# Last expert of a decoder step: two row additions moved, ye copied by halves, scatter and squares by tile

## The chip, the cores and the metric

The kernel runs on one core of a Trainium2 chip. The metric is the device time of one execution in microseconds (us); lower is better. The runs of the kernel before are shown by their median and spread; the profile is of one further execution, which has a time of its own.

## The reference, cut to what matters

One inference step of a two-layer decoder trunk over 256 prompt tokens and 32 sample tokens (288 rows of 1024 numbers, float32). Only its last part is touched: the expert feed-forward of layer 1 and the final norm.

```python
def moe_swiglu(x, w_router, w_gate, w_up, w_down):
    logits = (x @ w_router).astype(jnp.float32)
    top_val, top_idx = lax.top_k(logits, TOP_K_EXPERTS)          # 2 of 8
    gate = jax.nn.softmax(top_val, axis=-1)
    combine = jnp.einsum('btk,btke->bte', gate, one_hot(top_idx, N_EXPERTS))
    for e in range(N_EXPERTS):                                    # D_FF = 2816
        out = out + combine[..., e:e + 1] * swiglu(x, w_gate[e], w_up[e], w_down[e])
x = x + moe_swiglu(rms_norm(x, norm_ffn_odd), ...)
y = rms_norm(x, norm_final)
```

## The kernel before, in words

Everything up to the router runs first (attention, convolution, dense feed-forward, RWKV mixing) and is not touched. The experts then run one after the other, e = 0 to 7, inside a loop over blocks of `CAP` = 96 rows per expert; with these inputs the loop makes one round. Each engine has its own instruction stream, written out by hand, and semaphores tie them together.

**One expert on TensorE** (`expert` in the tensor block) has six phases, each over one weight matrix half (1408 of the 2816 hidden columns): gate0, up0, gate1 (three `widen`, L1589, output to banks 0 to 2 or 3 to 5), down0 (`narrow`, L1606, banks 6 and 7), up1 (`widen`), and down1 (`narrow`). Between up1 and down1 TensorE gathers the next expert's rows (`gather`, L1557); for the last expert it instead transposes the table `give` (L1647), which says which row belongs to which token and with what share. Weights stream through three buffers `part` of eight pieces each, loaded by SyncE (L723) as the pieces of the phase three back come free.

**VectorE and ScalarE**: for each of two halves, ScalarE takes silu of the gate product (`sg2`, L2013), and VectorE's `hidden` multiplies it by the up product (`hp`, L2615) and transposes it (`hidT`, L2619); `narrow` waits for each of the three groups of `hidT` in turn. At the expert's end both copy its 96 result rows from banks 6 and 7 to `ye`, ScalarE columns 0 to 511 (L2019) and VectorE columns 512 to 1023 (L2639), six pieces of 32x256 each.

**Results of experts 0 to 6** go from `ye` to a table `expert_rows` in device memory. When the seventh has been written, GpSimd fetches for every token tile (two tiles of 128 tokens, one of 32) its rows by an indirect DMA, six gathers in all, two per tile, into two buffers `got` (L2865). VectorE adds each to the running sum `acc` (`rows_in`, L2597); a gather starts when the addition two before it has freed its buffer. In the last expert all six additions stand on VectorE ahead of `hidden(…, 0)`.

**The last expert's result** is not sent through memory: TensorE's `scatter` (L1573) multiplies `ye` by the transposed `give`, in six steps g of one tile and one half of the columns, order tile 0 left, tile 0 right, tile 1 left, and so on, into banks 3 to 5 in turn; VectorE's `add_rows` (L2608) adds each to `acc`, and a step from the fourth on waits until its bank has been added. After the sixth addition ScalarE squares and sums the three tiles (L2033), loads the table of the square root (L2036), and VectorE scales the rows to `y_out` (L2703), which SyncE writes out (L748, L751).

Two semaphores matter: `ye_ok` counts the copies to `ye` (one from each engine per expert), `sc_ok` the additions of `add_rows` (with one more from before the loop). `mix_ok` belongs to the RWKV stage and has come to 48 long before.

Of the kernel before, what the change touches and what calls it, by code (L numbers as in the profile page):

```python
# [155 lines left out]
def build(nc, I, O):  # L156
# [235 lines left out]
    OUT_0 = 7  # L392
    OUT_1 = OUT_0 + 2
    N_OUT = OUT_1 + 1 + KC + 1


    ident_in, x_in, cst_in, vec_in, x2_in = (
# [28 lines left out]
    gu_mm, silu_ok, hid_ok, down_mm, down_ok = sem("gu_mm"), sem("silu_ok"), sem("hid_ok"), sem("down_mm"), sem("down_ok")  # L426


    xx_ok, mix_ok, lh_mm, lh_ok = (sem(n) for n in ("xx_ok", "mix_ok", "lh_mm", "lh_ok"))
    el_ok, mask_ok, cum_ok, e_ok, kf_ok = (sem(n) for n in ("el_ok", "mask_ok", "cum_ok", "e_ok", "kf_ok"))  # L430
    t1_ok, sqk_ok, hs_mm, nk_ok, nsq_ok, rn_ok = (sem(n) for n in ("t1_ok", "sqk_ok", "hs_mm", "nk_ok", "nsq_ok", "rn_ok"))
    kk_mm, kk_ok, ab_ok, kd_ok, rr_ok = (sem(n) for n in ("kk_mm", "kk_ok", "ab_ok", "kd_ok", "rr_ok"))
# [323 lines left out]
    def _(pe):  # L756
# [340 lines left out]
        rms_pe(pe, 1, sq2)  # L1097
        h_in = [(0, HD), (1, HD), (2, P)]
        for i, r in h_in:
            pe.wait_ge(mix_ok, KC * (i + 1))  # L1100
            w = weights(pe, n0 + i)[:, 0:KC * r].rearrange("p (k n) -> p k n", k=KC)
            for k in range(KC):
                last = mm(bk[5 + i][0:r, 0:T], w[:, k], mx[:, i % 2, k], start=k == 0, stop=k == KC - 1)  # L1103
            last.then_inc(lh_mm, 1)
# [14 lines left out]
        def krv_job(j):  # L1119
            i = j // KC  # L1120
            pe.wait_ge(job_ok, NIN + max(j - 1, 24))
            pe.wait_ge(mix_ok, KC * (i + 1))
            project(pe, n0 + 3 + j - 24, mx[:, i % 2], bk[6 + j % 2][:, 0:T]).then_inc(job_mm, 1)

        for j in range(24, 33):
# [435 lines left out]

        def scatter(blk, g):

            if g == 0:
                pe.wait_ge(ye_ok, blk * (2 * NE) + 2 * NE)
                pe.wait_ge(gt_ok, blk + 1)
            if g >= 3:
                pe.wait_ge(sc_ok, blk * 6 + 1 + g - 2)
            i, half = g // 2, g % 2
            t0, tn = TILES[i]  # L1570
            for q in range(tn // 32):
                at = 32 * (q + half * (i == 2))
                last = mm(up_bk[g % 3][at:at + 32, :], giveT[:, t0 + 32 * q:t0 + 32 * q + 32],  # L1573
                          ye[:, 512 * half:512 * half + 512], start=True, stop=True)
            last.then_inc(sc_mm, 1)
# [39 lines left out]
        def expert(blk, e):  # L1615

            def gate0_k(k):
                if k == 0:
                    pe.wait_ge(xe_ok, blk * (2 * NE) + 2 * e + 2)

            def up0_k(k):
                if k == 0 and e == 0:
                    pe.wait_ge(sc_ok, blk * 6 + 1)

            def gate1_k(k):
                if k == 0:
                    pe.wait_ge(silu_ok, blk * (6 * NE) + FC + 6 * e + 3)

            def up1_k(k):
                if k == 0:  # L1630
                    pe.wait_ge(hid_ok, blk * (6 * NE) + FC + 6 * e + 3)

            widen(blk, e, 0, gate_bk, gu_mm, gate0_k)
            widen(blk, e, 1, up_bk, up_mm, up0_k)
            widen(blk, e, 2, gate_bk, gu_mm, gate1_k)
            if e:
                pe.wait_ge(ye_ok, blk * (2 * NE) + 2 * e)
            narrow(blk, e, 3, 0)
            widen(blk, e, 4, up_bk, up_mm, up1_k)

            pe.wait_ge(silu_ok, blk * (6 * NE) + FC + 6 * e + 6)
            pe.wait_ge(pick_ok, blk * NE + e + 2)
            if e < NE - 1:
                gather()
            else:
                for i, (t0, tn) in enumerate(TILES):
                    last = nc.tensor.transpose(gate_bk[2][0:CAP, t0:t0 + tn], give[0:tn, i], C["ident"][0:tn, 0:tn])  # L1647
                last.then_inc(gt_mm, 1)
            narrow(blk, e, 5, 1)
# [15 lines left out]
    def _(act):  # L1665
# [340 lines left out]
        def expert(blk, e):  # L2006
            for half in range(2):
                for g in range(3):
                    n = 6 * e + 3 * half + g
                    act.wait_ge(gu_mm, blk * (6 * NE) + FC + n + 1)  # L2010
                    if n >= 3:
                        act.wait_ge(hid_ok, blk * (6 * NE) + FC + n - 2)
                    nc.scalar.activation(sg2[:, g], gate_bk[g][:, 0:FQ], ACT.Silu).then_inc(silu_ok, 1)  # L2013
            act.wait_ge(down_mm, blk * (2 * NE) + FC + 2 * e + 2)
            if e:
                act.wait_ge(rows_out, blk * (16 * LAST) + 16 * e)
            for q in range(2):
                for g in range(3):
                    last = nc.scalar.copy(ye[32 * g:32 * g + 32, 256 * q:256 * q + 256],  # L2019
                                          down_bk[g // 2][32 * q:32 * q + 32, 256 * (g % 2):256 * (g % 2) + 256])  # L2020
            last.then_inc(ye_ok, 1)
            if e < LAST:
                act.wait_ge(ye_ok, blk * (2 * NE) + 2 * e + 2)
                act.dma_start(expert_rows[CAP * e:CAP * e + CAP, :], ye[:]).then_inc(rows_out, 16)

        act.wait_ge(blocks_ok, 1)
        n_blocks = act.value_load(blocks[0:1, 0:1], min_val=1, max_val=T // CAP)
        with act.Fori(0, n_blocks) as blk:
            for e in range(NE):
                expert(blk, e)  # L2030
        act.wait_ge(sc_ok, n_blocks * 6 + 1)
        for i, (t0, tn) in enumerate(TILES):
            last = nc.scalar.activation(y_out[0:tn, i], acc[0:tn, i], ACT.Square, accum_out=ssf[0:tn, i:i + 1])  # L2033
        last.then_inc(sq_ok, 1)
        act.wait_ge(ms_ok, 3)
# [4 lines left out]
    def _(dve):  # L2040
# [223 lines left out]
        def mixed(i, m):  # L2264
            for c in range(KC):
                v_ = VEC["mu"] + KC * m + c
                V.scalar_tensor_tensor(mx[:, i % 2, c], xx[:, c], vecT[:, v_:v_ + 1], xn2[:, c],
                                       ALU.mult, ALU.add).then_inc(mix_ok, 1)

        for i, m in enumerate((1, 4, 5, 2, 0)):  # L2270
            if i >= 2:
# [314 lines left out]
                                       share[r, i, bass.ds(blk * NE + e, 1)], ALU.is_equal, ALU.mult)  # L2586
            return last

        def rows_in(blk):

            for n in range(6):
                i, j = n // 2, n % 2
                tn = TILES[i][1]
                dve.wait_ge(rows_back[j], blk * 48 + 16 * i + 16)
# [5 lines left out]
        def add_rows(blk):  # L2600
            dve.wait_ge(spot_then_rows, blk * 7 + 7)
            for g in range(6):
                i, half = g // 2, g % 2
                tn = TILES[i][1]
                dve.wait_ge(sc_mm, blk * 6 + g + 1)
                a = acc[0:tn, i, 512 * half:512 * half + 512]
                at = 32 * half * (i == 2)
                V.tensor_tensor(a, up_bk[g % 3][at:at + tn, :], a, ALU.add).then_inc(sc_ok, 1)  # L2608
# [11 lines left out]

        def expert(blk, e):
            if e == LAST:
                rows_in(blk)
            hidden(blk, e, 0)
            if e == LAST:
                gives(blk, e)
            picks(blk, e + 1).then_inc(pick_ok, 1)
            hidden(blk, e, 1)
            if e < NE - 1:
                columns_in(blk, e + 1)  # L2630
# [3 lines left out]
            if e:  # L2634
                dve.wait_ge(rows_out, blk * (16 * LAST) + 16 * e)
            dve.wait_ge(down_mm, blk * (2 * NE) + FC + 2 * e + 2)
            for q in range(2, 4):
                for g in range(3):
                    last = V.tensor_copy(ye[32 * g:32 * g + 32, 256 * q:256 * q + 256],  # L2639
                                         down_bk[g // 2][32 * q:32 * q + 32, 256 * (g % 2):256 * (g % 2) + 256])  # L2640
            last.then_inc(ye_ok, 1)

        dve.wait_ge(rank_mm, 1)
        V.scalar_tensor_tensor(rank[:, 0:2, 0:NE], bk[0][:, 0:2 * NE].rearrange("p (i e) -> p i e", i=2), 1.0, sel[:, 0:2],
# [40 lines left out]
            last = V.tensor_copy(share[0:NS, 2, NE * b:NE * b + NE], comb[0:NS, 2])  # L2685
        link(last)
        dve.wait_ge(gn_pool, gp_at["acc1"])
        V.tensor_copy(blocks_f[0:1, 3:4], blocks_f[0:1, 1:2]).then_inc(sc_ok, 1)
        dve.wait_ge(blocks_ok, 1)
        n_blocks = dve.value_load(blocks[0:1, 0:1], min_val=1, max_val=T // CAP)  # L2690
        with dve.Fori(0, n_blocks) as blk:
# [216 lines left out]
```

## Time and profile before

| | |
|---|---|
| median of 3 runs | 1580.28 us (1578.26 to 1580.69) |
| the profiled execution | 1587.68 us, span of its instructions 1585.8 us |
| TensorE (PE) matmul busy | 1498.8 us, 95% of the span |
| VectorE (DVE), ScalarE (ACT), GpSimd (POOL) busy | 442.2, 220.9, 164.7 us |
| mean granted TensorE clock | 0.969 of full speed |
| DMA over the whole span | 384.86 MB, 243 GB/s |
| chain that ended last, by engine | PE 85%, DVE 9%, DMA 3%, ACT 1%, issue 1% |
| costliest group | L1589 matmul, 6144 instructions, 459.1 us |

The chain is the work that ended last, followed back from the end: at each step to what released it. Matmul records overlap, so the time of a stretch is read from starts, not from a sum of durations. "[2.81 <-DVE ye L2639]" behind a row says that the engine was idle for 2.81 us before it and what ended the idle time.

### The profile page before, as it was taken

What the parts mean: (1) busy time and instruction counts of PE and PEld (TensorE: products, weight loads), DVE (VectorE), ACT (ScalarE), POOL (GpSimd) and SP (SyncE); (2) the same over time, 40 slices, a digit from 0 to 9 for tenths busy, and PEclk for the clock granted to TensorE, in tenths of its full rate; (3) what the DMA queues carried; (4) which work ended last, traced back from release to release, by engine and by line L of the source; (5) the groups of instructions that cost most, each with busy time, mean ns of one, the idle gap of its engine ahead of it and who ended that gap; (6) DMA issues with size and microseconds to landing.
All of it is one profiled execution on the core that took longest, in us unless ns stands there. A gap on an engine that the chain in (4) does not pass through costs nothing.

```text
span 1585.8 us, 39125 instructions
## 1 busy us (share of the span) xinstructions
PE 1498.8 (95%) x17804; PEld 974.7 (61%) x17804; DVE 442.2 (28%) x962; ACT 220.9 (14%) x479; POOL 164.7 (10%) x208
## 2 busy tenths in 40 slices
PE   6999989999995998999899999999999999999985
PEld 4767877777773777889764555545454555545432
DVE  1289321111006456353631011211111011211123
ACT  3134120000002511131330000000000000000001
POOL 3127200000000224105200000000000000000100
PEclk9899999999997999998899999999999999999997
DMA  9636034353531430032489999999999999999992
GB/s 286 189 126 163 14 108 157 109 159 112 180 107 53 134 93 2 3 56 56 100 308 362 414 413 413 374 415 375 413 387 395 414 371 413 370 415 374 403 399 73
DMA packets 187551, 384.86 MB, mean 243 GB/s; under 512 B 42463, under 2 KB 125631, under 8 KB 187258
## 3 DMA queue, kind: packets, MB, share of 16 engines
q1 hardware_dynamic: 180352, 365.84, 62.6%
q0 software_dynamic: 3616, 12.85, 2.1%
q10 hardware_dynamic: 3418, 3.68, 0.7%
q8 instruction: 140, 2.29, 0.6%
q14 instruction: 25, 0.20, 0.0%
HBM read 375.59 MB, written 6.73 MB: 241 GB/s over the span
## 4 chain that ended last, share of the span: by engine, by line
PE 85%; DVE 9%; DMA 3%; ACT 1%; issue 1%; SPq 0%; DVEq 0%; POOL 0%; ACTq 0%; POOLq 0%
PE bk L1589 26%; PE bk L1606 14%; PE bk L1076 11%; PE bk L761 8%; PE bk L1089 5%; PE bk L1510 2%; PE bk L1557 2%; PE bk L1169 2%; PE bk L991 2%; DMA got<-expert_rows,spot_now 2%; DMA ring<-in_w_in_even 1%; PE bk L1103 1%; DVE left L2158 1%; DVE tops L2156 1%; PE bk L1113 1%
## 5 line engine op out<-in xcount | busy, mean ns | idle before, releaser
L1589 PE MATMUL bk<-part,xe 128*32 128x352 f32 x6144 | 459.1, 460 | 2.3 <-DVE xe L2580 2.3
L1589 PEld LDWEIGHTS bk<-part,xe 128*32 128x32 f32 x6144 | 207.1, 110 | 249.0 <-issue 246.5
L1606 PE MATMUL bk<-part,hidT 128*32 128x256 f32 x4224 | 234.7, 382 | 5.7 <-DVE hidT L2619 5.7
L1606 PEld LDWEIGHTS bk<-part,hidT 128*32 128x32 f32 x4224 | 141.5, 111 | 97.1 <-DVE hidT L2619 8.9
L1076 PE MATMUL bk<-xn,ring 128*128 128x288 f32 x704 | 173.8, 411 | 3.2 <-DMA ring<-in_ffn_up 3.2
L2615 DVE TENSOR_TENSOR hp<-sg,bk 128x352 f32<-128x352 f32 x48 | 37.5, 781 | 470.8 <-PE bk L1589 470.8
L1076 PEld LDWEIGHTS bk<-xn,ring 128*128 128x128 f32 x704 | 135.4, 192 | 41.2 <-issue 3.4
L761 PE MATMUL bk<-xg,ring 128*128 128x288 f32 x336 | 90.4, 429 | 9.9 <-DMA ring<-in_w_in_even 8.3
L761 PE MATMUL bk<-mx,ring 128*128 128x288 f32 x384 | 96.2, 409 | 0.0
L1089 PE MATMUL bk<-hid,ring 128*128 128x288 f32 x352 | 85.5, 406 | 0.0
L761 PEld LDWEIGHTS bk<-xg,ring 128*128 128x128 f32 x336 | 66.5, 201 | 30.3 <-issue 9.1
L761 PEld LDWEIGHTS bk<-mx,ring 128*128 128x128 f32 x384 | 72.0, 190 | 20.4 <-issue 0.9
L1089 PEld LDWEIGHTS bk<-hid,ring 128*128 128x128 f32 x352 | 66.9, 190 | 18.5
L2864 POOL TENSOR_TENSOR free_now<-row_ss 128x1 f32 x5 | 1.0, 195 | 668.4 <-DMA expert_rows<-ye 650.6
L2019 ACT COPY ye<-bk 32x256 f32<-32x256 f32 x48 | 17.4, 362 | 369.9 <-PE bk L1606 369.4
L2013 ACT ACTIVATE sg<-bk 128x352 f32<-128x352 f32 x48 | 22.2, 464 | 319.9 <-PE bk L1589 283.5
L2639 DVE COPY ye<-bk 32x256 f32<-32x256 f32 x48 | 20.3, 424 | 98.9 <-PE bk L1606 98.4
L2238 DVE TENSOR_TENSOR gs<-bk,rs 128x288 f32<-128x288 f32 x22 | 10.1, 458 | 132.5 <-PE bk L1076 132.5
L2787 POOL MEMSET rmask<- 128x288 f32 x1 | 0.3, 338 | 325.2 <-DVE xn L654 325.2
L1510 PE MATMUL bk<-gT,ro 128*128 128x288 f32 x128 | 34.1, 422 | 0.0
L1557 PE MATMUL bk<-xr,pick 128*32 128x256 f32 x576 | 32.6, 379 | 1.4 <-ACT Ss L1960 1.4
L1794 ACT ACTIVATE sg<-gs 128x288 f32<-128x288 f32 x22 | 9.8, 444 | 155.8 <-DVE gs L2238 155.8
(512 smaller groups left out, 1368.6 us busy)
## 6 DMA issues: line engine op xcount, KB each, us to landing
part<-in_moe_gate SPq DMA_DIRECT2D x136, 704.0 KB, 7.3
part<-in_moe_up SPq DMA_DIRECT2D x136, 704.0 KB
part<-in_moe_down SPq DMA_DIRECT2D x128, 704.0 KB, 8.3
ring<-in_rwkv_w_rkv SPq DMA_DIRECT2D x24, 512.0 KB, 3.9
ring<-in_ffn_gate SPq DMA_DIRECT2D x22, 512.0 KB, 5.6
ring<-in_ffn_up SPq DMA_DIRECT2D x22, 512.0 KB, 6.7
ring<-in_ffn_down SPq DMA_DIRECT2D x22, 512.0 KB, 4.2
ring<-in_w_in_even SPq DMA_DIRECT2D x16, 512.0 KB, 5.9
```

The lines of the kernel that those rows point to most:

```text
L761: last = mm(out, w[:, k], rhs[:, k], start=k == 0, stop=k == KC - 1)
L991: last = nc.tensor.matmul(bk[4 + c // 2][:, TP * (c % 2):TP * (c % 2) + TP], w[:, k], mixT[:, k, 0:TP], start=k == 0 and c % 2 == 0, stop= ...
L1076: last = mm(bk[2 * m + f % 2][:, 0:T], slots[2 * m + k // 4][:, k % 4, (f % 2) * P:(f % 2 + 1) * P], xn1[:, k], start=k == 0, stop=k == KC ...
L1089: last = mm(bk[banks[c]][:, 0:T], w[:, f % 2, c * P:(c + 1) * P], hid[:, f], start=f == 0, stop=f == FC - 1)
L1169: last = mm(bk[GRP[q % 3][par]][r, hp * CH:(hp + 1) * CH], lhs[r, p2, par, hp], rhs[r, p2, par, hp], start=True, stop=True)
L1510: last = mm(bk[OUT_BANK(c)][:, 0:T], w[:, k], gT[:, k], start=k == 0, stop=k == KC - 1)
L1557: last = mm(gate_bk[g // 2][32 * q:32 * q + 32, 256 * (g % 2):256 * (g % 2) + 256], pick[:, i, 32 * g:32 * g + 32], in_parts[:, q], start= ...
L1589: last = mm(banks[g][32 * c:32 * c + 32, 0:FQ], xe[:, k, 32 * g:32 * g + 32], parts[ph % 3][:, FH * k + FQ * c:FH * k + FQ * c + FQ], star ...
L1606: last = mm(down_bk[g // 2][32 * q:32 * q + 32, 256 * (g % 2):256 * (g % 2) + 256], hidT[:, half, g, 32 * m:32 * m + 32], parts[ph % 3][:, ...
L2013: nc.scalar.activation(sg2[:, g], gate_bk[g][:, 0:FQ], ACT.Silu).then_inc(silu_ok, 1)
L2615: V.tensor_tensor(hp[:, g].rearrange("p (m j) -> p j m", m=NM), sg2[:, g].rearrange("p (j m) -> p j m", m=NM), up_bk[g][:, 0:FQ].rearrange ...
L2639: last = V.tensor_copy(ye[32 * g:32 * g + 32, 256 * q:256 * q + 256], down_bk[g // 2][32 * q:32 * q + 32, 256 * (g % 2):256 * (g % 2) + 256])
```

## The change

Five things, all in or behind the last expert.

1. `rows_in` takes a range: additions 0 to 3 (the two big tiles) stay ahead of `hidden(…, 0)`, additions 4 and 5 (the tile of 32) come behind `give` and `pick`, ahead of `hidden(…, 1)`.
2. `ye` is copied half by half: each engine copies three pieces of the left 512 columns and then three of the right (ScalarE the even quarters, VectorE the odd). `ye_ok` now counts the left half; the right half is counted on `mix_ok`, renamed `mix_then_ye`, above the 48 (`MIXED`) that it had. This holds for all eight experts.
3. `scatter` goes left half of tiles 0 and 1, then right half of both, then tile 2 (`SCATTER`). Its first step waits for the left half of `ye` alone, its third for the right.
4. The squares start tile by tile, when the third, fourth and sixth addition is done (`DONE_AT`).
5. A square root of eight numbers into a part of `y_out` that is overwritten later stands ahead of the squares. The count of `sc_ok` before the loop is 6 in place of 1.

```diff
+    SCATTER = ((0, 0), (1, 0), (0, 1), (1, 1), (2, 0), (2, 1))
+    MIXED = 6 * KC
+    DONE_AT = (3, 4, 6)
...
         def scatter(blk, g):
 
+            i, half = SCATTER[g]
             if g == 0:
+                pe.wait_ge(gt_ok, blk + 1)
                 pe.wait_ge(ye_ok, blk * (2 * NE) + 2 * NE)
-                pe.wait_ge(gt_ok, blk + 1)
+            if g == 2:
+                pe.wait_ge(mix_then_ye, blk * (2 * NE) + MIXED + 2 * NE)
             if g >= 3:
-                pe.wait_ge(sc_ok, blk * 6 + 1 + g - 2)
-            i, half = g // 2, g % 2
+                pe.wait_ge(sc_ok, blk * 6 + 6 + g - 2)
...
             if e:
                 pe.wait_ge(ye_ok, blk * (2 * NE) + 2 * e)
+                pe.wait_ge(mix_then_ye, blk * (2 * NE) + MIXED + 2 * e)
             narrow(blk, e, 3, 0)
...
-            for q in range(2):
+            for half in range(2):
+                q = 2 * half
                 for g in range(3):
                     last = nc.scalar.copy(ye[32 * g:32 * g + 32, 256 * q:256 * q + 256],
                                           down_bk[g // 2][32 * q:32 * q + 32, 256 * (g % 2):256 * (g % 2) + 256])
-            last.then_inc(ye_ok, 1)
+                last.then_inc((ye_ok, mix_then_ye)[half], 1)
             if e < LAST:
                 act.wait_ge(ye_ok, blk * (2 * NE) + 2 * e + 2)
+                act.wait_ge(mix_then_ye, blk * (2 * NE) + MIXED + 2 * e + 2)
...
         act.wait_ge(sc_ok, n_blocks * 6 + 1)
+        nc.scalar.activation(y_out[32:64, 2, 0:NE], C["slots"][32:64, 0:NE], ACT.Sqrt)
         for i, (t0, tn) in enumerate(TILES):
+            act.wait_ge(sc_ok, n_blocks * 6 + DONE_AT[i])
             last = nc.scalar.activation(y_out[0:tn, i], acc[0:tn, i], ACT.Square, accum_out=ssf[0:tn, i:i + 1])
...
-        def rows_in(blk):
-
-            for n in range(6):
+        def rows_in(blk, first, last_):
+
+            for n in range(first, last_):
...
             for g in range(6):
-                i, half = g // 2, g % 2
+                i, half = SCATTER[g]
...
             if e == LAST:
-                rows_in(blk)
+                rows_in(blk, 0, 4)
             hidden(blk, e, 0)
             if e == LAST:
                 gives(blk, e)
             picks(blk, e + 1).then_inc(pick_ok, 1)
+            if e == LAST:
+                rows_in(blk, 4, 6)
             hidden(blk, e, 1)
...
-            for q in range(2, 4):
+            for half in range(2):
+                q = 2 * half + 1
                 for g in range(3):
                     last = V.tensor_copy(ye[32 * g:32 * g + 32, 256 * q:256 * q + 256],
                                          down_bk[g // 2][32 * q:32 * q + 32, 256 * (g % 2):256 * (g % 2) + 256])
-            last.then_inc(ye_ok, 1)
+                last.then_inc((ye_ok, mix_then_ye)[half], 1)
...
-        V.tensor_copy(blocks_f[0:1, 3:4], blocks_f[0:1, 1:2]).then_inc(sc_ok, 1)
+        V.tensor_copy(blocks_f[0:1, 3:4], blocks_f[0:1, 1:2]).then_inc(sc_ok, 6)
```

How the instructions stand now. On VectorE, in the last expert, from the additions of gathered rows on; before (`acc<-got` is an addition of gathered rows, `hp` and `hidT` the first half's hidden columns):

```order
L2597 SCALAR_TENSOR_TENSOR acc<-got,weight,acc 128x1024
L2597 ISA
L2597 SCALAR_TENSOR_TENSOR acc<-got,weight,acc 32x1024
L2596 REGISTER_ALU
L2597 ISA
L2597 SCALAR_TENSOR_TENSOR acc<-got,weight,acc 32x1024
L2613 REGISTER_ALU
L2615 TENSOR_TENSOR hp<-sg_200,bk 128x32x11
L2619 STREAM_TRANSPOSE hidT<-hp 128x352
```

and in the change, from the fourth addition to the second half's first product:

```order
L2607 SCALAR_TENSOR_TENSOR acc<-got,weight,acc 128x1024
L2623 REGISTER_ALU
L2625 TENSOR_TENSOR hp<-sg_200,bk 128x32x11
L2629 STREAM_TRANSPOSE hidT<-hp 128x352
```

```order
L2578 TENSOR_SCALAR pick<-cst,rank,ssf 128x96
L2607 ISA
L2607 SCALAR_TENSOR_TENSOR acc<-got,weight,acc 32x1024
L2606 REGISTER_ALU
L2607 ISA
L2607 SCALAR_TENSOR_TENSOR acc<-got,weight,acc 32x1024
L2623 REGISTER_ALU
L2625 TENSOR_TENSOR hp<-sg_200,bk 128x32x11
```

The two additions of 32 rows have moved from ahead of the first half's three products to behind `give` and `pick`.

On ScalarE, from the last copies to `ye` to the end of its stream, with the semaphores that each instruction waits for; before:

```order
L2019 COPY ye<-bk 32x256 x5
L2028 REGISTER_ALU
L2028 COMPARE_AND_BRANCH
L2031 ISA
L2033 ACTIVATE y_out,ssf<-acc 128x1024 [waits sc_ok]
L2033 ACTIVATE y_out,ssf<-acc 128x1024
L2033 ACTIVATE y_out,ssf<-acc 32x1024
L2036 ACT_TABLE_LOAD
L2036 ACTIVATE ssf<-ssf 128x3 [waits ms_ok]
```

and in the change:

```order
L2026 COPY ye<-bk 32x256 x5
L2036 REGISTER_ALU
L2036 COMPARE_AND_BRANCH
L2039 ISA
L2040 ACT_TABLE_LOAD
L2040 ACTIVATE y_out<-cst 32x8 [waits sc_ok]
L2042 REGISTER_ALU
L2043 ACTIVATE y_out,ssf<-acc 128x1024 [waits sc_ok]
L2042 REGISTER_ALU
L2043 ACTIVATE y_out,ssf<-acc 128x1024 [waits sc_ok]
L2042 REGISTER_ALU
L2043 ACTIVATE y_out,ssf<-acc 32x1024 [waits sc_ok]
```

The table load has moved ahead of the squares, right behind the copies and itself without a wait, and no other load stands between the squares and the last square root.

## Rows read from the trace of the kernel before

**Rows 1.** The waits, 1400 to 1586 us: engine, line, waited for, us, times, longest

```profile
PE bk L1606 <- DVE hidT L2619: 5.7, 5, 4.0
PE bk L1573 <- DVE ye L2639: 2.8, 1, 2.8
```

**Rows 2.** The chain in order of time: start us, us, what

```profile
1419.02 14.24 PE bk L1606 x264
```

**Rows 3.** Instructions in order of time, TensorE: start us, us, engine, line, operation

```profile
1465.41 42.79 PE L1589 MATMUL bk<-part,xe 128*32 128x352 f32 x576
1512.15 0.89 PE L1606 MATMUL bk<-part,hidT 128*32 128x256 f32 x8 [3.95 <-DVE hidT L2619]
...
1514.64 15.83 PE L1606 MATMUL bk<-part,hidT 128*32 128x256 f32 x248 [0.15 <-DVE hidT L2619]
1530.30 14.37 PE L1589 MATMUL bk<-part,xe 128*32 128x352 f32 x192
```

**Rows 4.** Instructions in order of time, VectorE, last expert

```profile
1500.53 1.29 DVE L2597 SCALAR_TENSOR_TENSOR acc<-got,weight,acc 128x1024 f32<-128x1024 f32 x1 [1.82 <-DMA got<-expert_rows,spot_now]
...
1509.46 1.27 DVE L2597 SCALAR_TENSOR_TENSOR acc<-got,weight,acc 32x1024 f32<-32x1024 f32 x1 [1.58 <-DMA got<-expert_rows,spot_now]
1510.77 0.75 DVE L2615 TENSOR_TENSOR hp<-sg,bk 128x352 f32<-128x352 f32 x1
...
1515.19 0.79 DVE L2568 TENSOR_SCALAR pick<-cst,rank,ssf 128x96 f32<-128x96 f32 x3
```

**Rows 5.** Instructions in order of time, GpSimd: the last gather

```profile
1502.65 0.87 POOL L2865 DMA_INDIRECT got<-expert_rows,spot_now  x1 [0.46 <-issue]
```

**Rows 6.** Instructions in order of time, SyncE's queue, last weights; and the tile part, 1462 to 1586

```profile
1481.63 12.75 SPq L723 DMA_DIRECT2D part<-in_moe_up  x8
1495.83 12.75 SPq L723 DMA_DIRECT2D part<-in_moe_down  x8
...
DMA to landing us min/median/max: 6.0/13.2/15.2
```

**Rows 7.** Instructions in order of time, the end of the kernel

```profile
1561.24 2.61 DVE L2639 COPY ye<-bk 32x256 f32<-32x256 f32 x6 [13.37 <-PE bk L1606]
...
1563.98 7.67 PE L1573 MATMUL bk<-ye,giveT 96*32 96x512 f32 x36 [2.81 <-DVE ye L2639]
...
1566.05 0.69 DVE L2608 TENSOR_TENSOR acc<-bk,acc 128x512 f32<-128x512 f32 x1 [2.20 <-PE bk L1573]
1567.68 0.69 DVE L2608 TENSOR_TENSOR acc<-bk,acc 128x512 f32<-128x512 f32 x1 [0.94 <-PE bk L1573]
...
1570.87 2.20 DVE L2608 TENSOR_TENSOR acc<-bk,acc 128x512 f32<-128x512 f32 x3 [0.79 <-PE bk L1573]
...
1575.20 1.04 ACT L2033 ACTIVATE y_out<-acc 32x1024 f32<-32x1024 f32 x1
...
1576.35 1.28 ACT L2036 ACT_TABLE_LOAD   x1
1576.36 0.17 DVE L2698 TENSOR_SCALAR ssf<-ssf 128x3 f32<-128x3 f32 x1 [3.29 <-ACT y_out L2033]
1577.65 0.20 ACT L2036 ACTIVATE ssf<-ssf 128x3 f32<-128x3 f32 x1
```

**Rows 8.** Stretches: us, PE, PEld, DVE, ACT, POOL busy (instructions), PEclk, DMA share, GB/s

```profile
1512.00:1514.60 2.60, 1.97 (x16) 0.36 (x16) 2.53 (x6) 0.93 (x2) 0.00 (x0) 0.58 1.02 416
1514.60:1520.00 5.40, 5.36 (x60) 2.59 (x64) 1.38 (x6) 0.46 (x1) 0.00 (x0) 0.57 1.02 413
...
1564.00:1572.00 8.00, 7.65 (x36) 1.83 (x36) 3.08 (x5) 0.00 (x0) 0.00 (x0) 0.60 0.00 0
```

**Rows 9.** Other idle times of TensorE: instructions in order of time, then stretches

```profile
833.08 4.09 PE L1557 MATMUL bk<-xr,pick 128*32 128x256 f32 x72 [1.45 <-ACT Ss L1960]
...
839.47 0.96 PE L1589 MATMUL bk<-part,xe 128*32 128x352 f32 x8 [2.30 <-DVE xe L2580]
...
833.00:837.00 4.00, 3.92 (x72) 2.32 (x72) 0.00 (x0) 1.15 (x1) 0.00 (x0) 1.00 0.48 105
...
840.00:843.00 3.00, 3.00 (x24) 1.12 (x20) 0.00 (x0) 0.00 (x0) 0.00 (x0) 0.50 1.03 428
```

**Rows 10.** Instructions in order of time, ScalarE: a square behind a square root

```profile
771.71 0.22 ACT L1954 ACTIVATE gst<-gst 128x16 f32<-128x16 f32 x1 [1.03 <-DVE gst L2470]
...
805.11 0.60 ACT L1992 ACTIVATE bk<-xr 128x512 f32<-128x512 f32 x1
```

More of the change, by code:

```diff
@@ L426, in build @@
     gu_mm, silu_ok, hid_ok, down_mm, down_ok = sem("gu_mm"), sem("silu_ok"), sem("hid_ok"), sem("down_mm"), sem("down_ok")
-    xx_ok, mix_ok, lh_mm, lh_ok = (sem(n) for n in ("xx_ok", "mix_ok", "lh_mm", "lh_ok"))
+    xx_ok, mix_then_ye, lh_mm, lh_ok = (sem(n) for n in ("xx_ok", "mix_then_ye", "lh_mm", "lh_ok"))
     el_ok, mask_ok, cum_ok, e_ok, kf_ok = (sem(n) for n in ("el_ok", "mask_ok", "cum_ok", "e_ok", "kf_ok"))
@@ L1099, in _ @@
         for i, r in h_in:
-            pe.wait_ge(mix_ok, KC * (i + 1))
+            pe.wait_ge(mix_then_ye, KC * (i + 1))
             w = weights(pe, n0 + i)[:, 0:KC * r].rearrange("p (k n) -> p k n", k=KC)
@@ L1121, in krv_job @@
             pe.wait_ge(job_ok, NIN + max(j - 1, 24))
-            pe.wait_ge(mix_ok, KC * (i + 1))
+            pe.wait_ge(mix_then_ye, KC * (i + 1))
             project(pe, n0 + 3 + j - 24, mx[:, i % 2], bk[6 + j % 2][:, 0:T]).then_inc(job_mm, 1)
@@ L1622, in up0_k @@
                 if k == 0 and e == 0:
-                    pe.wait_ge(sc_ok, blk * 6 + 1)
+                    pe.wait_ge(sc_ok, blk * 6 + 6)
             def gate1_k(k):
@@ L2267, in mixed @@
                 V.scalar_tensor_tensor(mx[:, i % 2, c], xx[:, c], vecT[:, v_:v_ + 1], xn2[:, c],
-                                       ALU.mult, ALU.add).then_inc(mix_ok, 1)
+                                       ALU.mult, ALU.add).then_inc(mix_then_ye, 1)
         for i, m in enumerate((1, 4, 5, 2, 0)):
```

## The prediction

> **What bounds the kernel now.** I read the page first: TensorE is busy for 95% of the span and carries 85% of the chain, so time is won only where TensorE waits, or where it has nothing left to do. The waits come next, cut to the last two experts [rows 1]: TensorE waits 5.7 us in all for `hidT` and 2.8 us for `ye`. Then the chain and the instructions in order of time say what each wait costs.
>
> The first place is down0 of the last expert. TensorE's three widen phases start at 1465.41 and run 42.79 us, to 1508.20; down0's first matmul starts 3.95 us later, at 1512.15 [rows 3]. It waits for `hidT`, and VectorE was adding gathered rows: the fourth addition ends at 1501.82, the sixth starts at 1509.46, and only then, at 1510.77, comes the first product [rows 4]. The wait costs more than it shows. An undisturbed down0 takes 14.24 us [rows 2]; this one ends where up1 starts, at 1530.30 [rows 3]. From 1508.20 that is 22.10 us, 7.86 more. The rest is the clock: 0.58 and 0.57 of full speed are granted from 1512.00 to 1520.00 [rows 8], mostly the lower level (1.2 GHz) after the idle time.
>
> The second place is the end [rows 7]. VectorE copies `ye` for 2.61 us while TensorE is idle, the scatter takes 7.67 us at a mean clock of 0.60 [rows 8], the last three additions end at 1573.07, three squares follow one by one to 1576.33, then a table load of 1.28 us, a root, the scaling and the output. All of it is one chain.
>
> **Part 1, the two additions.** VectorE can start the first half's products at 1501.82 in place of 1510.77. They took from 1510.77 to about 1514.6, when TensorE's last group was released [rows 3, 4], 3.9 us; now they are done by 1505.7, 2.5 us before TensorE wants the first. So the stall goes whole: down0 runs 1508.20 to 1522.44 with the clock kept. **Gain 7.86 us.** What is late next? `give` and `pick` end about 1.5 us behind the products (14.6 to 15.98 in [rows 4]), so at 1507.2; addition 4 and 5 follow, the last not before its gather, issued at 1502.65 [rows 5], has landed at about 1509.4 as before [rows 4]. Those two gathers don't move: each starts when the addition two before it is done, and additions 2 and 3 stand where they were. Queued behind addition 5 on VectorE is the second half's work, which TensorE's up1 releases only at 1522.44 + 14.3 = 1536.7. That is 27 us of cover; if the cover went, each us of late gather would stop down1 by as much.
>
> The weights: TensorE now comes to up1 and down1 7.9 us sooner. up1's pieces are issued from 1481.63 in 12.75 us, down1's from 1495.83 in 12.75, and a piece lands at most 15.2 us behind its issue [rows 6]: up1's last by 1509.6, against 1522.4 when it is wanted; down1's by 1523.8, against 1536.7. Both hold, with 13 us. Cost nothing.
>
> **Part 2, `ye` by halves and the new scatter order.** Six copies take 2.61 us, three 1.31. In times of the profile before (shift all by 7.86), the left half is there at 1562.55 and the scatter starts at 1562.67, 1.31 us sooner than 1563.98 [rows 7]. What follows hangs on the clock.
> - At the lower level nothing else changes on TensorE: a scatter step of a big tile, 8 of the 36 matmuls, takes 7.67 x 8/36 = 1.70 us (the first two additions are 1.63 apart, [rows 7]), the additions follow at TensorE's pace, and the last ends 1.31 sooner, at 1571.76.
> - At the full level a step takes 0.85 us. The idle time is now 2.81 - 1.31 = 1.5 us. The trace has two idle times near it: after 1.45 us at 833.08 the clock stays 1.00, after 2.30 us at 839.47 it is 0.50 from 840.00 on [rows 9]. 1.5 is nearest to the first, so I take full speed. The first step's result is there 0.85 + 0.37 us after its start (0.37 is 2.07, from 1563.98 to the first addition at 1566.05, less 1.70), at 1563.9, just when VectorE has finished the right half of `ye` (1563.85). Additions come every 0.85 us, the fourth from 1566.45, the last two behind it at 0.73 each (2.20 for three, [rows 7]): the end is at 1568.6. The right half of `ye` is ready before step 3, so its wait costs nothing.
>
> **Part 3, squares by tile.** Tile 0 is whole after the third addition, so two squares of 1.04 us lie beside additions, and only tile 2's is left behind the last, 1.13 us with its read (1575.20 to 1576.33). Squares end at 1568.65 + 1.13 = 1569.8 at full speed, 1572.9 at the lower level, against 1576.33. **Gain of parts 2 and 3: 6.5 us, or 3.4 at the lower level.**
>
> **Part 4, the table.** The load moves right behind the copies of `ye`, where ScalarE has nothing else to do: its first square comes at about 1566.3, 2.5 us behind the last copy of VectorE, and the load takes 1.28. No square loads a table again: the square at 805.11 stands behind the root at 771.71 with no load between [rows 10], and the order of the changed stream has none. The root now waits for VectorE's 0.17 us alone: 1576.36 + 0.17 + 0.05 = 1576.58 in place of 1577.65 [rows 7]. **Gain 1.07 us.** The Trainium skill (ScalarE: Activation LUTs, What ACT_TABLE_LOAD costs) gives a switch some 1.28 us for the load and 1.38 for a drain, 2.66 in all. By it this term would be an estimated 2.4 us and the sum 1.4 larger. The trace agrees on the load and not on the rest: the root starts 0.02 us behind the load's end (1577.63), so there is no drain to save here, and I go by the row.
>
> **Part 5, what is added.** One more wait ahead of down0 on TensorE in seven experts, one in the scatter; one on ScalarE ahead of each write of `expert_rows`; three ahead of squares. TensorE's chain in a full expert has no idle time between gate1 and down0 (down0 runs its 14.24 us through as one piece of the chain, [rows 2]), and its sequencer is ahead of the array. Lower bound nothing; upper bound the 0.15 us of idle time that the shortest wait of [rows 3] shows, for eight waits 1.2 us. I take nothing, since a semaphore long reached stops nobody at the old wait beside it. That the left half's copies now read other columns costs nothing: same count, same size.
>
> **Sum.** 7.86 + 6.5 + 1.07 = 15.4 us (faster). The profiled execution took 1587.68, so 1572.3 for a profiled one like it. It stands 7.40 above the median, so the same difference is taken off the median: 1580.28 - 15.4 = **1564.9 us**.
>
> **Rivals.**
> - *The scatter stays at 1.2 GHz.* For: the idle time remains at its head, and after 2.30 us the clock fell. Against: 1.45 us kept it. Sum 7.86 + 3.4 + 1.07 = 12.3, 1568.0 us. The Trainium skill (TensorE: Matmul & The Clock Gate, Why this matters for your kernels) asks only that long idle gaps between bursts be avoided, longer ones than any here. By that rule this rival has no chance; but the trace shows the lower level behind 2.30 and behind 2.81 us already, so the rule does not settle 1.5.
> - *The stall comes back in another form.* The weights are late for up1 or down1, as DMA is at a share of 1.02 all through the stretch [rows 8], and what TensorE wins in down0 it waits later. Then parts 2 to 4 alone count: 7.6 us, 1572.7. Against it stand 13 us of margin.
> - *The first part's gain is smaller in the runs shown than in the profile.* 3.95 us of it is idle time and 3.9 is clock; how long the lower level lasts may differ between executions. With half of the clock's share the sum is 13.5, 1566.8 us.
> - *Slower.* The added wait ahead of down0 stands in all of the experts from the second on, seven times, in the phase boundary of the engine that bounds. If reading a second semaphore cost TensorE more than 15.4/7 = 2.2 us each, the kernel would lose; 2.7 us would make it 1583.8. Nearest price for it is 0.15 us, and VectorE's longest idle time for issue alone is below 2 us. That is very unlikely.
> - *The change does not do what it says*: the squares wait anyway, or a second table load returns. The order excludes the second; the first would return 2.1 us, 1567.0.
>
> **Chances.** Full speed and all parts 0.55; lower level in the scatter 0.22; smaller first part, or squares late, 0.15; weights late 0.05; 0.03 is left for no gain or a loss, 0.02 of it slower by over 0.2% and 0.01 within. The forecast is 1564.9. The range of 8 in 10 reaches over these but the last two: low 1562.5 (the skill's drain, or 2.4 us of spread as the three runs show), high 1569.0 (lower level with 1 us for the added waits). A change of 0.2%, 3.2 us, is about the least that a measurement of this kernel can tell from none. Faster 0.97, within it 0.01, slower 0.02.
>
> **What the profile after would show.** No idle time of TensorE ahead of the last down0, and clock 1.00 there; the six row additions with the three products between the fourth and the fifth; the scatter starting 1.5 us behind down1's last matmul, and lasting about 4.1 us (the prediction of part 2 is wrong if it is 7.7 with a clock near 0.6); the first square before the last addition; one load ahead of the squares and a root 0.05 us behind VectorE's 0.17. The whole is wrong if TensorE waits at up1 or down1 for DMA, or if phases of experts 1 to 6 have grown.

## The result, and the profile after

| | before | changed |
|---|---|---|
| median, same chip (6 runs each) | 1580.49 us (1576.74 to 1584.68) | 1565.91 us (1561.48 to 1567.21) |
| ratio, 95% interval | | 0.9904 (0.9884 to 0.9924) |
| profiled execution, its span | 1587.68, 1585.8 us | 1567.21, 1565.3 us |
| mean granted TensorE clock | 0.969 | 0.978 |

The kernel is 15.2 us faster by the ratio (12.0 to 18.3), 14.6 by the medians. The forecast was 1564.9 (1562.5 to 1569.0), a gain of 15.4. The change was run again beside the experiments: 0.9928 (0.9905 to 0.9951) and 0.9918 (0.9902 to 0.9934). As gains, the three ratios are 15.2, 11.4 and 13.0 us: all inside the range of the forecast (11.3 to 17.8), and all below its centre.

The two profiled executions are 20.5 us apart, which is more than either the forecast or the ratio. The first lines to read are therefore the start of the expert loop in the chains. After:

```profile
834.77 44.50 PE bk L1594 x576
879.27 14.24 PE bk L1611 x264
...
1503.50 14.24 PE bk L1611 x264
1517.74 13.06 PE bk L1594 x176
```

Before, the first expert's phases start at 839.47 [rows 9], after at 834.77: 4.7 us of the difference lie in stages that the change does not touch. The start moves as much without any edit: in two further profiles of the changed kernel it is 838.96 and 833.51. Only stretches within one trace are compared from here on. From that start to the end of the span it was 1585.8 - 839.47 = 746.3 us and is 1565.3 - 834.77 = 730.5: **15.8 us** won.

TensorE in the last expert, in order of time (start us, us, engine, line, operation), after:

```profile
1460.71 42.79 PE L1594 MATMUL bk<-part,xe 128*32 128x352 f32 x576
1503.31 14.43 PE L1611 MATMUL bk<-part,hidT 128*32 128x256 f32 x264
1517.55 14.39 PE L1594 MATMUL bk<-part,xe 128*32 128x352 f32 x192
...
1549.90 4.63 PE L1578 MATMUL bk<-ye,giveT 96*32 96x512 f32 x36 [1.49 <-DVE ye L2652]
```

down0 now follows gate1 with nothing between. I call M1 the time from the first gate0 matmul to the first of up1: 1530.30 - 1465.41 = 64.89 us before [rows 3], 56.84 after. The clock, in stretches (us, PE, PEld, DVE, ACT, POOL busy, PEclk, DMA share, GB/s):

```profile
1503.00:1517.00 14.00, 14.00 (x264) 8.73 (x260) 1.65 (x2) 0.89 (x2) 0.00 (x0) 1.00 1.02 406
1549.50:1554.50 5.00, 4.60 (x36) 1.48 (x36) 4.40 (x9) 3.77 (x8) 0.00 (x0) 1.00 0.00 0
```

1.00 in both, where [rows 8] had 0.57, 0.58 and 0.60. VectorE in the same expert shows why, in order of time:

```profile
1495.53 1.28 DVE L2607 SCALAR_TENSOR_TENSOR acc<-got,weight,acc 128x1024 f32<-128x1024 f32 x1 [1.80 <-DMA got<-expert_rows,spot_now]
1496.84 0.80 DVE L2625 TENSOR_TENSOR hp<-sg,bk 128x352 f32<-128x352 f32 x1
...
1500.24 0.55 DVE L2629 STREAM_TRANSPOSE hidT<-hp 128x352 f32<-128x352 f32 x1
...
1502.11 1.27 DVE L2607 SCALAR_TENSOR_TENSOR acc<-got,weight,acc 32x1024 f32<-32x1024 f32 x1
1504.46 1.27 DVE L2607 SCALAR_TENSOR_TENSOR acc<-got,weight,acc 32x1024 f32<-32x1024 f32 x1 [1.08 <-DMA got<-expert_rows,spot_now]
```

The products come right behind the fourth addition and the last `hidT` is there at 1500.79, 2.5 us before TensorE starts down0. The last addition ends at 1505.73 with 25 us to spare. The end of the kernel, in order of time:

```profile
1548.48 2.62 DVE L2652 COPY ye<-bk 32x256 f32<-32x256 f32 x6 [13.37 <-PE bk L1611]
...
1550.81 1.28 ACT L2040 ACT_TABLE_LOAD   x1
...
1551.13 1.45 DVE L2618 TENSOR_TENSOR acc<-bk,acc 128x512 f32<-128x512 f32 x2
...
1553.60 2.19 DVE L2618 TENSOR_TENSOR acc<-bk,acc 128x512 f32<-128x512 f32 x3 [0.17 <-PE bk L1578]
...
1555.82 1.05 ACT L2043 ACTIVATE y_out<-acc 32x1024 f32<-32x1024 f32 x1 [0.17 <-DVE acc L2618]
...
1557.20 0.20 ACT L2046 ACTIVATE ssf<-ssf 128x3 f32<-128x3 f32 x1 [0.23 <-DVE ssf L2711]
1557.65 3.67 DVE L2716 SCALAR_TENSOR_TENSOR y_out<-acc,ssf,gain_f 128x1024 f32<-128x1024 f32 x3
```

I call M2 the time from VectorE's first copy to `ye` to its first scaling of `y_out`, which before was

```profile
1578.09 3.66 DVE L2703 SCALAR_TENSOR_TENSOR y_out<-acc,ssf,gain_f 128x1024 f32<-128x1024 f32 x3
```

So M2 is 1578.09 - 1561.24 = 16.85 us before [rows 7] and 9.17 after. From up1 to the copies it is 30.94 and 30.93, behind the first scaling 7.7 both times. From the first expert's first gate0 matmul to the last expert's it is 625.94 us in both. So the 15.8 us are 8.05 (M1), 7.68 (M2), and 0.07 of rest, which is less than the 0.1 us to which a span is given.

### The profile page after: what moved, and what is told of

Read it like the earlier page. It is cut to its first block, busy times and chain, and to the rows that moved or that the text cites. A ratio compares the mean times of both kernels' runs of the same rounds, so it can differ in the third digit from the quotient of the medians.

```text
span 1565.3 us, 39145 instructions
## 1 busy us (share of the span) xinstructions
PE 1486.4 (95%) x17804; PEld 971.0 (62%) x17804; DVE 442.2 (28%) x962; ACT 220.3 (14%) x480; POOL 164.5 (11%) x208
## 4 chain that ended last, share of the span: by engine, by line
PE 87%; DVE 9%; DMA 1%; ACT 1%; issue 1%; SPq 0%; DVEq 0%; ACTq 0%
PE bk L1594 29%; PE bk L1611 15%; PE bk L1079 11%; PE bk L764 8%; PE bk L1092 5%; PE bk L1513 2%; PE bk L1560 2%; PE bk L1172 2%; PE bk L994 2%; DMA ring<-in_w_in_even 1%; DVE left L2168 1%; PE bk L1106 1%; DVE tops L2166 1%; PE bk L1116 1%; DVE kT L2340 1%
## 5 line engine op out<-in xcount | busy, mean ns | idle before, releaser
L1611 PE MATMUL bk<-part,hidT 128*32 128x256 f32 x4224 | 231.4, 379 | 1.2 <-DVE hidT L2629 1.2
```

Source lines behind the costliest of these rows:

```text
L1611: last = mm(down_bk[g // 2][32 * q:32 * q + 32, 256 * (g % 2):256 * (g % 2) + 256], hidT[:, half, g, 32 * m:32 * m + 32], parts[ph % 3][:, ...
```

## The experiments

Every ratio is to the kernel before on the same chip. Where one execution is named, the stretches of its trace are all that is read. The first four kernels ask whether the stall went because the additions moved, and whether idle time is what sets the clock in the scatter.

**All six additions first again.** The change without part 1:

```diff
-                rows_in(blk, 0, 4)
+                rows_in(blk, 0, 6)
...
-            if e == LAST:
-                rows_in(blk, 4, 6)
```

> The change without its first part: all six additions of gathered rows stand ahead of the last expert's first products again. Two stretches of the run's own trace are read. M1, from the last expert's first gate0 matmul to its first up1 matmul, was 64.9 us before and 56.8 in the change. M2, from VectorE's first copy to ye to its first scaling of y_out, was 16.9 us before and 9.2 in the change. My theory (the products queued behind additions 5 and 6, and the lower clock after that idle time): M1 back at 61.5 to 65 with 4 us of idle time ahead of down0, M2 stays 9.2, so the time is some 8 us above the change and 7.6 below before, ratio to before 0.995. Rival (the stall went because of the copies by halves or the shifted transfers, not because of the additions): M1 stays 57 and the ratio 0.990.

Measured: 1572.81 us, ratio 0.9958 (0.9944 to 0.9971). M1 65.01, M2 9.17. TensorE in order of time:

```profile
1459.91 42.79 PE L1594 MATMUL bk<-part,xe 128*32 128x352 f32 x576
1506.71 0.78 PE L1611 MATMUL bk<-part,hidT 128*32 128x256 f32 x8 [4.01 <-DVE hidT L2629]
...
1509.21 15.88 PE L1611 MATMUL bk<-part,hidT 128*32 128x256 f32 x248 [0.16 <-DVE hidT L2629]
1524.92 14.37 PE L1594 MATMUL bk<-part,xe 128*32 128x352 f32 x192
```

The idle time is back at 4.01 us and with it the long down0. M1 came out at the top end that was given.

**Part 1 alone, in the kernel before.**

```diff
-                rows_in(blk)
+                rows_in(blk, 0, 4)
...
             picks(blk, e + 1).then_inc(pick_ok, 1)
+            if e == LAST:
+                rows_in(blk, 4, 6)
```

> The kernel before with the first part of the change alone. My theory: the parts are additive, M1 56.8 and M2 16.9, time 8.0 us below before, ratio 0.995. Rival (down0 coming sooner collides with the weight stream or the gathers, and only the rest of the change makes room): M1 above 58 or an idle time of TensorE in up1 or down1 that ends with a DMA, ratio 0.997 or more.

Measured: 1571.61 us, ratio 0.9942 (0.9925 to 0.9959). M1 56.84, as forecast; no wait of TensorE in up1 or down1 ends with a DMA. M2 is 15.36 and not 16.9, with every instruction of that stretch as before: the scatter behind the same 2.81 us of idle time took 6.33 us, not 7.67 [rows 7]. In the profile before, the lower level holds from before the scatter's start at 1563.98 to about 1570.4; here the scatter starts at full speed, the lower level comes at about 1551.4 and goes at about 1554.8.

```profile
1460.13 42.79 PE L1589 MATMUL bk<-part,xe 128*32 128x352 f32 x576
1502.73 14.43 PE L1606 MATMUL bk<-part,hidT 128*32 128x256 f32 x264
1516.97 14.39 PE L1589 MATMUL bk<-part,xe 128*32 128x352 f32 x192
...
1550.63 6.33 PE L1573 MATMUL bk<-ye,giveT 96*32 96x512 f32 x36 [2.81 <-DVE ye L2641]
```

**The scatter waits for both halves.**

```diff
             if g == 0:
                 pe.wait_ge(gt_ok, blk + 1)
                 pe.wait_ge(ye_ok, blk * (2 * NE) + 2 * NE)
-            if g == 2:
                 pe.wait_ge(mix_then_ye, blk * (2 * NE) + MIXED + 2 * NE)
```

> The change, but the scatter's first step waits for both halves of ye; order of steps, copies and squares as changed. My theory (idle time decides the clock): 2.8 us of idle time ahead of the scatter, then the lower level: scatter 7 to 7.7 us at a mean clock near 0.6, M2 = 9.2 + 1.3 + 3.1 = 13.6. Rival (VectorE's additions bound the scatter and the clock does not matter to them): scatter at most 5 us between first and last addition, M2 = 10.5.

**The same, with TensorE busy meanwhile.** On top of it:

```diff
                 pe.wait_ge(gt_ok, blk + 1)
+                for n in range(4):
+                    for c in range(4):
+                        mm(gate_bk[0][32 * c:32 * c + 32, 0:FQ], xe[:, n, 0:32], hidT[:, 0, 0], start=True, stop=True)
                 pe.wait_ge(ye_ok, blk * (2 * NE) + 2 * NE)
```

> As the run before it (scatter waits for both halves of ye), with 16 matmuls of 352 columns, their result unused, issued into a free bank while TensorE waits: some 2.4 us of work in the 2.8 us. If the idle time is what lowers the clock: scatter at clock 1.00 in about 4.5 us, M2 = 9.2 + 1.3 = 10.5. If the full wait itself slows the scatter in another way: the clock falls or the scatter is 7 us all the same, M2 near 13.6.

Measured, one execution each. M2 was 12.15 with the idle time and 10.44 with the matmuls in it. Its two ends on VectorE, TensorE's scatter and the scatter's stretch, first with the idle time:

```profile
1550.03 2.62 DVE L2651 COPY ye<-bk 32x256 f32<-32x256 f32 x6 [13.37 <-PE bk L1610]
...
1562.18 3.67 DVE L2715 SCALAR_TENSOR_TENSOR y_out<-acc,ssf,gain_f 128x1024 f32<-128x1024 f32 x3
```

```profile
1552.71 6.34 PE L1577 MATMUL bk<-ye,giveT 96*32 96x512 f32 x36 [2.74 <-DVE ye L2651]
```

```profile
1552.80:1559.10 6.30, 6.25 (x36) 1.55 (x36) 2.95 (x5) 2.18 (x5) 0.00 (x0) 0.73 0.00 0
```

and with it filled:

```profile
1548.05 2.62 DVE L2654 COPY ye<-bk 32x256 f32<-32x256 f32 x6 [13.37 <-PE bk L1613]
...
1558.49 3.66 DVE L2718 SCALAR_TENSOR_TENSOR y_out<-acc,ssf,gain_f 128x1024 f32<-128x1024 f32 x3
```

```profile
1547.80 2.55 PE L1572 MATMUL bk<-hidT,xe 128*32 128x352 f32 x32
1550.72 4.64 PE L1580 MATMUL bk<-ye,giveT 96*32 96x512 f32 x36 [0.37 <-DVE ye L2654]
```

```profile
1550.50:1554.50 4.00, 3.78 (x34) 1.29 (x36) 2.31 (x5) 1.58 (x3) 0.00 (x0) 1.00 0.00 0
```

The scatter starts at the same distance from the copies (2.68 and 2.67 us) and takes 4.64 us at full speed or 6.34 at a mean of 0.73. So the full wait costs 1.27 us by itself (10.44 against 9.17), and the idle time a further 1.71 through the clock. The first number was forecast (1.3). The second was put at 3.1, because the profile before happened to show a longer spell at the lower level; so M2 with the idle time missed its 13.6 by 1.45 us, and lies between my theory and the rival's 10.5. That it was the idle time and not the full wait itself rests on one execution of each kind. The other profiles agree: the clock fell in all three that have 2.7 to 2.8 us of idle time ahead of the scatter, this one among them, and in none of the nine that have 1.5 us.

**The change itself, as a reference.**

> The changed kernel once more, as it is, as the reference point on the same chip for the run that changes the output. Expected: ratio to before 0.990, M1 56.8, M2 9.2.

Measured: 1570.88 us, ratio 0.9928 (0.9905 to 0.9951), M1 56.85, M2 9.18. The ratio's centre is 3.8 us off the first, these two stretches 0.01 us: for effects of a few microseconds I read the stretches, not the times.

**The root without its early table load.**

```diff
-        nc.scalar.activation(y_out[32:64, 2, 0:NE], C["slots"][32:64, 0:NE], ACT.Sqrt)
```

> The change without the early square root, so that the table is loaded behind the squares again. My theory (the load's 1.28 us less VectorE's 0.17 beside it): from the end of the last square to the root's start 1.5 us in place of 0.23 plus 0.2, M2 = 9.2 + 1.1 = 10.3. The Trainium skill's cost of a switch with its drain: M2 = 11.6. Rival (the early load delays something that this run gives back): M2 below 10.

Measured, one execution: M2 10.25. ScalarE in order of time:

```profile
1556.53 0.18 ACT L2042 ACTIVATION_READ_ACCUMULATOR y_out<-acc 32x1 f32 x1
1556.73 1.28 ACT L2045 ACT_TABLE_LOAD   x1
1558.02 0.20 ACT L2045 ACTIVATE ssf<-ssf 128x3 f32<-128x3 f32 x1
```

1.08 us is what hiding the load is worth; nothing stands between load and root. The Trainium skill (ScalarE: Activation LUTs, What ACT_TABLE_LOAD costs) agrees on the load with its 1.28 us; its drain of 1.38 us does not appear here.

**All squares last.**

```diff
-    DONE_AT = (3, 4, 6)
+    DONE_AT = (6, 6, 6)
```

> The change, but every square waits for the sixth addition. My theory: two squares of 1.04 us come back behind the additions, M2 = 9.2 + 2.1 = 11.3, additions unchanged. Rival (squares beside additions slow the additions down, since both work on the same tile of memory): the additions take less than the 4.66 us of the change and M2 is below 10.8.

Measured, one execution: M2 11.25, so the two squares beside additions are worth 2.08 us.

```profile
1550.27 2.62 DVE L2652 COPY ye<-bk 32x256 f32<-32x256 f32 x6 [13.37 <-PE bk L1611]
...
1561.52 3.66 DVE L2716 SCALAR_TENSOR_TENSOR y_out<-acc,ssf,gain_f 128x1024 f32<-128x1024 f32 x3
```

The additions run from 2.65 to 7.30 us behind the first copy with or without squares beside them; the rival is out.

**Tile 1's output from ScalarE's queue.**

```diff
-        for n in range(KC):
+        for n in range(KC // 2):
...
+        act.wait_ge(fin_ok, 2)
+        for q in range(4):
+            landed_, base, step = piece_in(1, 2 * q)
+            act.wait_ge(landed_, n_blocks * (2 * NE * step) + (base + step))
+            act.dma_start(O["y_prompt"][0, P:2 * P, 256 * q:256 * q + 256],
+                          y_out[:, 1, 256 * q:256 * q + 256]).then_inc(out_done, 16)
```

> The change, and the four output transfers of tile 1 are issued by ScalarE's queue, which is idle, in place of SyncE's. In the change eight issues of 0.47 us each run one after the other from 1559.06 to 1562.83, the ninth for the 32 rows follows at 1562.88, though the last row is scaled at 1561.3; from the first scaling to the end of the span it takes 7.65 us. If issuing bounds the end: 6.2 to 6.7 us, 1.0 to 1.5 us faster than the change. If the transfers themselves bound it (DMA share 0.81 there): 7.3 us or more, within 0.4 us of the change.

Measured: 1569.62 us, ratio 0.9914 (0.9887 to 0.9940), not to be told from the change beside it. The last issue ends 4.5 us behind the first scaling in place of 5.7, but the end comes 7.56 us behind it, against 7.65 to 7.73 in the three profiles of the change. So issuing does not bound the end. That the transfers do fits the DMA share, which is 0.73 to 1.36 in every half microsecond from 1562.5 to 1566.5; no run isolates it from the time that a single transfer needs to land.

**Matmuls in the first expert's wait.** The finding on the clock, carried to another place:

```diff
+                if k == 0 and e == 0:
+                    in_parts = xr[:, 0].rearrange("p (k q d) -> p q k d", k=KC, q=4)
+                    for n in range(18):
+                        c = n % 4
+                        mm(down_bk[0][32 * c:32 * c + 32, 0:256], pick[:, 0, 0:32], in_parts[:, c], start=True, stop=True)
                 if k == 0:
                     pe.wait_ge(xe_ok, blk * (2 * NE) + 2 * e + 2)
```

> The change, and TensorE gets 18 matmuls of 256 columns, their result unused, while it waits 2.3 us for the first expert's columns. In the change the three widen phases behind that wait take 44.50 us, in every other expert 42.60. If idle time is what lowers the clock, here as at the end: the three phases take 42.6, first gate0 matmul no later, 1.9 us won in this stretch and nothing elsewhere (M1 56.8, M2 9.2). If the 1.9 us come from something else, say the first weights landing late: 44.5 again.

Measured, one execution: the three phases take 42.81 us, the chain's row of the change has 44.50; M1 is 56.85 and M2 9.17. The stretches of the first microseconds, with the matmuls:

```profile
834.00:838.00 4.00, 3.84 (x56) 1.62 (x52) 0.57 (x2) 0.00 (x0) 0.00 (x0) 1.00 0.99 401
```

and in the change:

```profile
834.80:838.00 3.20, 3.20 (x28) 1.36 (x32) 0.00 (x0) 0.00 (x0) 0.00 (x0) 0.58 1.00 414
```

But the change, run again as a reference, shows this row, with no matmuls added:

```profile
838.96 42.81 PE L1594 MATMUL bk<-part,xe 128*32 128x352 f32 x576 [2.30 <-DVE xe L2590]
```

The same 2.30 us of idle time, and the clock stayed (1.00 in the 4 us behind it). Of the eleven profiles whose wait there was left as it is, those of the kernel before and of the change among them, it fell in ten and stayed in this one. So this one execution does not prove by itself that the matmuls kept the clock; the next kernel has them too and shows 42.81 again, which makes two of two with them and one of eleven without.

**All together.** The matmuls, tile 1's output on ScalarE, and tile 0 scaled in two halves (the waits of the two output queues, not shown, are moved to match):

```diff
-        for i, (t0, tn) in enumerate(TILES):
-            V.scalar_tensor_tensor(y_out[0:tn, i], acc[0:tn, i], ssf[0:tn, i:i + 1], gain_f[0:tn], ALU.mult,
-                                   ALU.mult).then_inc(fin_ok, 1)
+        for i, h0, h1 in ((0, 0, 512), (0, 512, D), (1, 0, D), (2, 0, D)):
+            tn = TILES[i][1]
+            V.scalar_tensor_tensor(y_out[0:tn, i, h0:h1], acc[0:tn, i, h0:h1], ssf[0:tn, i:i + 1], gain_f[0:tn, h0:h1],
+                                   ALU.mult, ALU.mult).then_inc(fin_ok, 1)
```

> All that might add to the change: the matmuls in the first expert's wait, tile 1's output issued by ScalarE's queue, and tile 0 scaled in two halves of 512 columns so that its transfers start earlier. Expected: three phases 42.6 in place of 44.5; the first transfer issued 0.6 us sooner behind the first scaling, and the end 7.56 - 0.6 = 7.0 us behind it, since the transfers bound it. Together 2.5 us faster than the change: ratio to before 0.989 on average over chips, which timing alone can hardly tell from the change's 0.9904. If issue and landing hide it: end 7.5 again.

> The changed kernel as it is, on the same chip as the run before it. Expected: ratio to before 0.9905, M1 56.8, M2 9.2, end 7.65 behind the first scaling.

Measured: 1563.76 us (1559.19 to 1565.47), ratio 0.9898 (0.9880 to 0.9917); the change on the same chip 1565.95 (1564.81 to 1567.31), ratio 0.9918 (0.9902 to 0.9934). For the change, M1 is 56.85 and M2 9.17, as expected. The phases take 42.81 us, and the end comes 7.15 us behind the first scaling in place of 7.73. By the stretches that is 1.7 + 0.6 = 2.3 us, and the medians differ by 2.2; the intervals overlap, so the times alone do not show it. First scaling and first output transfer, with all together:

```profile
1554.85 3.79 DVE L2728 SCALAR_TENSOR_TENSOR y_out<-acc,ssf,gain_f 128x512 f32<-128x512 f32 x4
1555.72 1.81 SPq L751 DMA_DIRECT2D out_y_prompt<-y_out  x4
```

and in the first profile of the change:

```profile
1557.65 3.67 DVE L2716 SCALAR_TENSOR_TENSOR y_out<-acc,ssf,gain_f 128x1024 f32<-128x1024 f32 x3
1559.06 3.77 SPq L751 DMA_DIRECT2D out_y_prompt<-y_out  x8
```

The first transfer is issued 0.54 us sooner (0.87 against 1.41 behind the first scaling). Against the run that only moved tile 1's output (7.56) the end is 0.41 us sooner, so part of the 0.6 belongs to that move.

## Why the prediction was right, point by point

| term | forecast | measured in the traces | run that isolates it |
|---|---|---|---|
| part 1, stall ahead of down0 | 7.86 | 8.05 | 8.17 (back in), 8.05 (alone) |
| parts 2 and 3, scatter and squares | 6.5 | 6.60 (5.11 against part 1 alone) | see below |
| part 4, table load | 1.07 | 1.09 | 1.08 |
| part 5, added waits | 0 | 0.00 in the experts | |
| sum, with 0.07 of rest | 15.4 | 15.8 (14.3) | |

- **Part 1** held in its mechanism. Its price was 0.19 us too small. The step from 1465.41 over 42.79 us "to 1508.20" took the modelled end of the last matmul for the start of the next phase. Read from starts, as in full experts, it is 42.60, to 1508.01. A full expert before, from the chain in order of time, ahead of the row in [rows 2]:

```profile
1376.42 42.60 PE bk L1589 x576
```

- **How part 1's price splits** was wrong. The prediction counted 3.95 us of idle time and said "The rest is the clock", 3.9 us. But the second and third group of `hidT` came late too, and at any clock TensorE could not have started the third before 1514.64 [rows 3]. An estimate from these rows: at an undisturbed pace (264 matmuls in 14.24 us) the first 16 take 0.86 us, so waiting for VectorE cost 1514.64 - 1508.01 - 0.86 = 5.77 us; the other 248 would take 13.38 and took 15.66, so the lower clock cost 2.28. With the additions put back it is 5.84 and 2.33.
- **What is late next**: nothing. The first half's products were done 2.5 us early, as forecast, and the weights were never late: no wait on a DMA in up1 or down1, in the change or with part 1 alone. That rival is out.
- **Parts 2 and 3.** The scatter started 1.32 us sooner behind the copies (forecast 1.31), at full speed. It took 4.63 us where I had written 4.1. The additions ended 7.31 us behind the first copy, which is where the forecast had them (1568.6 - 1561.24 = 7.4), and squares 8.49 (8.6). Taken apart: 1.27 us for the earlier start, 2.08 for the squares, and 3.25 of the 6.60 are left for the clock; by itself that was measured only with the shorter spell, at 1.71. Against the trace with part 1 alone, which has the shorter spell, the squares' end gives 5.11 in place of 6.60, and 1.76 are left for the clock. So the term of 6.5 agrees with one profile, and its 3.1 us of clock are the longer of two spells seen.
- **The rival with the scatter at 1.2 GHz** did not come about. The run with both halves waited for shows what it would look like, but at 1.71 us for the clock, where the rival had 3.1. The idle times that the rival compares are those of the scatter and of the first expert; the one ahead of down0 was longer, 3.95 us.
- **The rival of a smaller first part in the runs shown** had a sound reason, since spells at the lower level do differ, as the scatter shows, 7.67 against 6.33 us for the same instructions. For the stall itself both traces that have it agree (64.89 and 65.01), so there it is not seen, and by the split above half of the clock's share would be 1.1 us and not 1.95.
- **The slower rival**, reading a second semaphore: three phases 42.60 and down0 14.24 us in the last expert as in a full one before, and 625.94 us from the first expert's start to the last's in both kernels, with six of the seven added waits inside. It costs nothing visible.
- **The step from the profile to the median** took the sum off the median as it stands. For the 4.7 us more that the profiled execution before had ahead of the experts that was right: a comparison of the two profiled totals, 20.5 us, would have overstated the gain by a third. For the scatter it was luck in part. The sum was read from an execution with a mean clock of 0.969, where the 34 timed runs of the kernel before beside the experiments have 0.971 to 0.978, and it took over the long spell. With the shorter one the stretches give 14.3 us, and the three ratios give 15.2, 11.4 and 13.0. How often either spell comes was not measured, so how much of the distance to 15.4 it explains stays open.

## What to carry to other kernels

In a stream that one engine works off in order, put work that waits for a transfer behind the work that the bounding engine waits for, and count what its wait costs twice: once as time until the last late piece is there, and once as clock afterwards (5.8 and 2.3 us here). Split the two by rows, since the idle time that is printed is neither. At the end of a kernel, where everything is one chain, start each consumer when its own half or tile is there, and load tables while the engine has nothing to do. Gains of some microseconds are best read from stretches of the same trace, which repeated to 0.1 us here wherever the clock was the same, while the times of one kernel's runs on one chip spread over up to 9 us. The same stretch under another spell of the clock differed by 1.3 to 1.7 us, so look at the clock of every stretch that is compared.

## What was not expected of the hardware

- The same instructions behind the same idle time can get either level of the clock. Behind 2.30 us in the first expert it fell in ten profiles and stayed at full speed in one, worth 1.7 us. Behind 2.7 to 2.8 us the scatter took 7.67 us once and 6.33 and 6.34 the other times. Behind 1.5 us at the end it stayed in all nine profiles that have that idle time. Where the line lies was not measured.
- Idle time filled with matmuls whose result nobody reads went with full speed at both places where it was tried (one execution at the scatter, two in the first expert), for 1.7 us each.
- Moving half of the output to an idle queue ended the issuing 1.2 us sooner and brought 0.1 us at most; starting the first transfer 0.54 us sooner on top of that brought 0.41.
